# Experts with first key 96 or more: one pass of 128-expert tiles in place of gathered rows

## The reference

```
q = (hf @ w_q).reshape(n_tok, 8, 2, 128)
half_scores = einsum('thpd,hpnd->thpn', q, sub_keys)        # 8 heads, 2 x 128 keys
s_top, i_top = top_k(half_scores, 16)
cand = s_top[:, :, 0, :, None] + s_top[:, :, 1, None, :]    # 16 x 16 pairs
cand_idx = i_top[:, :, 0, :, None] * 128 + i_top[:, :, 1, None, :]
best, pos = top_k(cand, 16);  expert_idx = cand_idx at pos;  gates = softmax(best)
act = einsum('td,thkd->thk', x, u_tab[expert_idx])
out = einsum('thk,thkd->td', gates * gelu(act), v_tab[expert_idx])
```

## Time and profile before

| | us |
|---|---|
| median of 3 runs | 2410.4 (2410.38 to 2410.79) |
| profiled execution | 2410.53 |
| its span, first to last instruction | 2408.9 |
| VectorE busy | 1360.5 (56%) |
| TensorE matmuls busy | 1545.4 (64%) |
| GpSimd busy | 564.1 (23%) |
| ScalarE busy | 186.3 (8%) |
| moved by DMA | 796.21 MB, mean 331 GB/s |

### The profile page before, as it was taken

One profiled execution on the slowest core, in us unless ns is written; L12 is line 12 of the kernel. 1 busy time (PEld: TensorE's weight loads), 2 busy tenths in 40 slices (PEclk: granted clock), 3 DMA queues, 4 the chain that ended last, 5 costly groups with the idle time before them and its releaser, 6 DMA issues.

```text
span 2408.9 us, 18981 instructions
## 1 busy us (share of the span) xinstructions
PE 1545.4 (64%) x7056; PEld 975.7 (41%) x7056; DVE 1360.5 (56%) x2094; ACT 186.3 (8%) x311; POOL 564.1 (23%) x552
## 2 busy tenths in 40 slices
PE   5899899989999999898233333333334333333335
PEld 4788788878888888786000000000000000000001
DVE  7821587794354412488766566566665555455543
ACT  1122221210000000200000000000000000000000
POOL 1000000000000000023444333334344433333342
PEclk9999899999999999999555555555555555555555
DMA  9963455656566564077999999999999999999996
GB/s 393 413 259 114 194 226 234 258 230 255 233 267 255 209 244 157 35 304 282 373 421 422 421 421 421 421 422 421 421 422 421 422 422 422 421 421 421 420 422 279
DMA packets 95343, 796.21 MB, mean 331 GB/s; under 512 B 11424, under 2 KB 11424, under 8 KB 13872
## 3 DMA queue, kind: packets, MB, share of 16 engines
q0 software_dynamic: 78512, 606.14, 61.1%
q1 hardware_dynamic: 16768, 189.27, 20.1%
HBM read 791.18 MB, written 4.19 MB: 330 GB/s over the span
## 4 chain that ended last, share of the span: by engine, by line
DMA 42%; PE 39%; DVE 12%; issue 4%; POOL 1%; ACT 1%; SPq 0%; POOLq 0%; DVEq 0%
DMA arena<-expert_u,expert 39%; PE ps L606 24%; PE ps L614 9%; DVE arena L1168 6%; PE ps L630 3%; DMA arena<-expert_v,expert_q 2%; DVE mod_rows L928 1%; DMA arena<-ada_early 1%; POOL arena L413 1%; DVE work L984 1%; DVE work L981 1%; DVE work L891 0%; PE ps L769 0%; PE ps L807 0%; POOL mod_rows L413 0%
## 5 line engine op out<-in xcount | busy, mean ns | idle before, releaser
L1168 DVE CUSTOM_DVE_ANT_0 arena<-arena,buf_b 128x2048 f32<-128x2048 f32 x256 | 586.2, 2293 | 481.3 <-DMA arena<-expert_u,expert 479.7
L819 PE MATMUL ps<-arena,mod_rows 128*32 128x512 f32 x1536 | 365.2, 1047 | 591.3 <-DMA arena<-expert_v,expert_q 562.9
L413 POOL DMA_INDIRECT arena<-expert_u,expert x256 | 255.5, 998 | 895.0 <-DVE work L1168 681.7
L606 PE MATMUL ps<-buf_a,arena 128*128 128x256 f32 x1920 | 423.9, 383 | 6.1 <-DVE arena L1002 5.3
L819 PEld LDWEIGHTS ps<-arena,mod_rows 128*32 128x32 f32 x1536 | 40.1, 140 | 908.1 <-DMA arena<-expert_v,expert_q 803.5
L606 PEld LDWEIGHTS ps<-buf_a,arena 128*128 128x128 f32 x1920 | 367.3, 192 | 57.2 <-issue 6.7
L819 PE MATMUL ps<-mod_rows 128*32 128x512 f32 x512 | 120.1, 1032 | 179.6 <-DMA mod_rows<-expert_v,expert_q 179.6
L606 PE MATMUL ps<-arena 128*128 128x256 f32 x1024 | 223.7, 379 | 1.0 <-ACT arena L545 1.0
L413 POOL DMA_INDIRECT arena<-expert_v,expert_q x192 | 199.6, 1039 | 80.5 <-issue 63.5
L606 PEld LDWEIGHTS ps<-arena 128*128 128x128 f32 x1024 | 193.9, 190 | 27.3 <-issue 1.3
L400 POOL DMA_DIRECT2D arena<-ada_late x32 | 16.9, 529 | 772.4 <-DVE mod_rows L928 642.6
(11 more groups left out here) (208 smaller groups left out, 1004.5 us busy)
## 6 DMA issues: line engine op xcount, KB each, us to landing
arena<-weights SPq DMA_DIRECT2D x62, 2048.0 KB, 7.9
arena<-ada_late POOLq DMA_DIRECT2D x32, 2048.0 KB, 9.2
arena<-ada_early SPq DMA_DIRECT2D x16, 2048.0 KB, 17.1
arena<-w_early SPq DMA_DIRECT2D x8, 1536.0 KB, 8.9
arena<-expert_u,expert POOLq DMA_INDIRECT x256, 16.8
arena<-expert_v,expert_q POOLq DMA_INDIRECT x192, 18.0
buf_a<-x_t SPq DMA_DIRECT2D x1, 2048.0 KB, 20.5
arena<-ln_rows POOLq DMA_DIRECT2D x1, 2048.0 KB, 7.2
```

Source lines behind the costliest of these rows:

```text
L413: pool.indirect_dma_start(slots[row % ring], None, table, bass.IndirectOffsetOnAxis(ap=indices[:, n // HEADS, column:column + 1], axis=0))\
L606: last = mm(ps[:, bank, c * TOKENS:(c + 1) * TOKENS], ring[slot][:, first + k, c * P:(c + 1) * P], rhs[:, k, :], start=(k == 0), stop=(k = ...
L819: last = mm(ps[j * GROUP:(j + 1) * GROUP, n // HEADS * QUADS + g, :], spread_w[n % 2][:, e, :], v_slot[row % V_RING][:, j * QCOLS:(j + 1) ...
L1168: v.tensor_tensor_reduce(out=u_slot[s], in0=u_slot[s], in1=h2[:, n // HEADS], scale=1.0, scalar=0.0, op0=ALU.mult, op1=ALU.add, accum_out= ...
```

## The change

Experts whose first key is 96 or more (4096 of 16,384, 32 tiles of 128) are no longer gathered. The gathers get `bounds_check=GATHERED - 1`, so a row with a larger index is left out and the slot keeps what it held; its gate is zero in `gates_left`, which `weigh` now reads. The products of `reduce_row` no longer go over the slot but to `products`, and each `reduce_row` waits for the one before.

- **U, dense.** SyncE streams 32 tiles of 1 MB of a transposed copy `dense_u` through two slots. `dense_u_piece` multiplies a quarter of a tile with all 256 tokens (4 matmuls, 128 x 128 by 256); a whole tile's result goes through Gelu on ScalarE into `dense_act`. Four tiles come ahead of the first weights, 28 are spread over queries 1 to 5.
- **Gates.** In queries 6 to 8 the chosen keys and gates are transposed by TensorE and copied by ScalarE, so that a token is a column. For each token a column mask (second key and gate; even tokens on ScalarE, odd ones on VectorE) and a row mask (first key, 16 tokens in one instruction) are multiplied by a matmul of 32 columns (`spread_gates`), which gives the token's gates over the 32 x 128 dense experts. `weigh_dense` multiplies `dense_act` by them, 16 tokens at a time.
- **V, dense.** 32 tiles of V are streamed through the same two slots, and `dense_v_piece` adds a quarter of a tile's product (8 matmuls) in queries 10 to 14 into the same eight PSUM banks.
- **Moved.** Block 1's choices are in queries 1 to 5 (`late_choices` walks through the same `choice`, two pieces ahead of the gates of the head before). Block 0's layer norm is in query 15. The stores of `x_mid` go from SyncE's queue to GpSimd's, ahead of the gathers. `xq` is loaded after the last dense U tile. V's ring has six slots instead of eight, and its gathers follow in their order from the sixth row of query 1 on. `pe.wait_ge(s_dw, BATCHES)` holds TensorE in front of its step 9.

TensorE's loop variable n now is one above that of the rows of V which it weighs.

```diff
-U_RING, V_RING = 4, 8
+U_RING, V_RING = 4, 6
+DENSE = 32
+FIRST_DENSE = N_KEYS - DENSE
+GATHERED = FIRST_DENSE * N_KEYS
+BATCH = 512 // DENSE
+BATCHES = TOKENS // BATCH
+MASKS = 8
...
         buf_a = sb("buf_a", [P, CHUNK])
         h_t = buf_a[:].rearrange("p (k t) -> p k t", k=KT)
...
         u_slot = [arena[:, s * row:(s + 1) * row] for s in (4, 5, 6, 7)]
-        v_slot = [arena[:, s * row:(s + 1) * row] for s in (8, 9, 10, 11)] + [shift2, scale2]\
-            + [arena[:, s * row:(s + 1) * row] for s in (0, 1)]
+        v_slot = [arena[:, s * row:(s + 1) * row] for s in (8, 9, 10, 11)] + [shift2, scale2]
+        dense_slot = [arena[:, s * row:(s + 1) * row] for s in (2, 3)]
+        dense_act = [buf_a[:].rearrange("p (a t) -> p a t", t=TOKENS), arena[:, 0:CHUNK].rearrange("p (a t) -> p a t", t=TOKENS)]
         late_scores = gate1.rearrange("p (c n) -> p c n", c=2 * HEADS)
+        col_mask = gate1[:, 0:MASKS * N_KEYS].rearrange("p (r n) -> p r n", r=MASKS)
...
         level_mask = cst[:, C_LEVELS:C_IOTA]
...
+        gates_left = part(BLOCKS * SLOTS).rearrange("p (b s) -> p b s", b=BLOCKS)
+        col_t = part(TOKENS)
+        distance = [pq_t[1][:, n * N_KEYS:(n + 1) * N_KEYS] for n in range(2)]
+        products = [xr[:, 1], sk.rearrange("p c n -> p (c n)")]
...
+        EARLY_DENSE = 4
+        FIRST_MASKS = 6
+        late_steps = [(n, e) for n in range(1, 6) for e in range(1, TOPK, 2)]
+        dense_steps = [(n, e) for n in range(1, 6) for e in range(TOPK)]
+        mask_steps = [(n, e) for n in range(FIRST_MASKS, HEADS + 1) for e in range(TOPK)]
+        v_steps = [(n, e) for n in range(HEADS + 2, 2 * HEADS - 1) for e in range(TOPK)]
...
+        DENSE_U_AT = shares(dense_steps, 4 * EARLY_DENSE, 4 * DENSE)
+        DENSE_V_AT = shares(v_steps, 0, 4 * DENSE)
+        TOKENS_AT = {(FIRST_MASKS + t * 3 // BATCH // TOPK, t * 3 // BATCH % TOPK): [] for t in range(TOKENS)}
+        for t in range(TOKENS):
+            TOKENS_AT[FIRST_MASKS + t * 3 // BATCH // TOPK, t * 3 // BATCH % TOPK].append(t)
+        SOFT_AT = {late_steps[5 * h + 3]: [h] for h in range(HEADS)}
...
+            for a in range(DENSE):
+                sp.wait_ge(dense_used[a % 2], 1 + a // 2)
+                sp.dma_start(dense_slot[a % 2], dense_u[a * P:(a + 1) * P, :]).then_inc(dense_loaded[a % 2], 16)
+            sp.wait_ge(s_mid, 16 * BLOCKS)
+            for s in range(2):
+                sp.wait_ge(dense_used[s], 1 + DENSE // 2)
+            for j in range(QUADS):
+                sp.dma_start(xq[j * GROUP:(j + 1) * GROUP].rearrange("t b g c -> t (b g) c"),
+                             x_mid.rearrange("(a t) (j c) -> j t a c", t=GROUP, j=QUADS)[j]).then_inc(s_xq, 16)
+            for a in range(DENSE, 2 * DENSE):
+                sp.wait_ge(dense_used[a % 2], 1 + a // 2)
+                sp.dma_start(dense_slot[a % 2], expert_v[GATHERED + (a - DENSE) * P:GATHERED + (a - DENSE + 1) * P, :])\
+                    .then_inc(dense_loaded[a % 2], 16)
+            sp.wait_ge(s_gmm, TOKENS)
...
-            for b in range(BLOCKS):
-                sp.wait_ge(s_x1, b + 1)
-                sp.dma_start(x_mid[b * P:(b + 1) * P, :], xr[:, b]).then_inc(s_mid, 16)
-            sp.wait_ge(s_mid, 16 * BLOCKS)
...
+                                        bass.IndirectOffsetOnAxis(ap=indices[:, n // HEADS, column:column + 1], axis=0),
+                                        bounds_check=GATHERED - 1, oob_is_err=False)\
...
+            for b in range(BLOCKS):
+                pool.wait_ge(s_x1, b + 1)
+                pool.dma_start(x_mid[b * P:(b + 1) * P, :], xr[:, b]).then_inc(s_mid, 16)
...
-            wait_alone(pool, used[0], 1 + F_END[0])
-            for e in range(V_RING - 2, V_RING):
-                gather_v(0, e)
...
-                    if n > 1 or e >= V_RING:
+                    if n > 1 or e >= (TOPK - U_RING) // 2:
...
-                gelu(i)
-                nc.scalar.preload_act_table_set("natural_log_exp_and_others")
-                soft_exp(i + (HEADS + 1))
-                nc.scalar.preload_act_table_set("gelu_and_others")
...
-            nc.scalar.preload_act_table_set("gelu_and_others")
-            with me.loop(HEADS - 1, 0) as i:
-                gelu(i + (HEADS + 1))
+            def dense_gelu(a):
+                act_e.wait_ge(dense_used[a % 2], 2 + a // 2)
+                run(dense_act[a // 16][:, a % 16, :], ps[:, 4 + a % 2, 0:TOKENS], ACT.Gelu).then_inc(s_dact, 1)
...
+                t = slice(b * P, (b + 1) * P)
+                act_e.wait_ge(s_tok, b + 1)
+                run(row_t[:, t], ps[:, 6, 0:P], ACT.Copy)
+                run(col_t[:, t], ps[:, 6, P:2 * P], ACT.Copy)
+                run(minus_col_t[:, t], ps[:, 6, P:2 * P], ACT.Copy, scale=-1.0)
+                run(gate_t[:, t], ps[:, 6, 2 * P:3 * P], ACT.Copy)
...
+                if t >= MASKS:
+                    act_e.wait_ge(s_gmm, t - MASKS + 1)
+                act_e.wait_ge(s_slot, t // P + 1)
+                me.link(run(distance[t // 2 % 2], keys, ACT.Abs, bias=minus_col_t[:, t:t + 1]))
+                run(col_mask[:, t % MASKS], distance[t // 2 % 2], ACT.Relu, bias=gate_t[:, t:t + 1], scale=minus_gate_t[:, t:t + 1])\
+                    .then_inc(s_col, 1)
+            for n in range(BLOCKS * HEADS):
+                for e in range(TOPK):
+                    for h in SOFT_AT.get((n, e), ()):
+                        nc.scalar.preload_act_table_set("natural_log_exp_and_others")
+                        soft_exp(HEADS + h + 1)
+                        nc.scalar.preload_act_table_set("gelu_and_others")
+                    if n == FIRST_MASKS and e == 0:
+                        for b in range(BLOCKS):
+                            choice_by_slot(b)
+                    for a in DENSE_U_AT.get((n, e), ()):
+                        if a % 4 == 3:
+                            dense_gelu(a // 4)
+                    for t in TOKENS_AT.get((n, e), ()):
+                        if t % 2 == 0:
+                            mask_cols(t)
+                    if n == BLOCKS * HEADS - 1 and e == 13:
+                        nc.scalar.preload_act_table_set("natural_log_exp_and_others")
+                        rstd_of_groups(0, 0, QUADS)
+                        nc.scalar.preload_act_table_set("gelu_and_others")
+                if n == 0:
+                    for a in range(EARLY_DENSE):
+                        dense_gelu(a)
+                gelu(n)
             nc.scalar.preload_act_table_set("natural_log_exp_and_others")
             for g in range(QUADS):
                 rstd_of_groups(1 + g, QUADS + g, QUADS + g + 1)
...
+            def dense_u_piece(i):
+                a, q = i // 4, i % 4
+                if q == 0:
+                    pe.wait_ge(dense_loaded[a % 2], 16 * (a // 2 + 1))
+                    if a > 1:
+                        pe.wait_ge(s_dact, a - 1)
+                tile = dense_slot[a % 2].rearrange("p (k j) -> p k j", k=KT)
+                for k in range(4 * q, 4 * q + 4):
+                    last = mm(ps[:, 4 + a % 2, 0:TOKENS], tile[:, k, :], h2_t[:, k, :], start=k == 0, stop=k == KT - 1)
+                if q == 3:
+                    last.then_inc(dense_used[a % 2], 1)
...
+                a, q = i // 4, i % 4
+                t = DENSE + a
+                if q == 0:
+                    pe.wait_ge(dense_loaded[t % 2], 16 * (t // 2 + 1))
+                for r in range(2 * q, 2 * q + 2):
+                    for j in range(QUADS):
+                        last = mm(ps[j * GROUP:(j + 1) * GROUP, r, :], dense_act[a // 16][:, a % 16, r * GROUP:(r + 1) * GROUP],
+                                  dense_slot[t % 2][:, j * QCOLS:(j + 1) * QCOLS], start=False, stop=False, skip_group_check=True)
+                if i == 4 * DENSE - 1:
+                    last.then_inc(s_dv, 1)
+                elif q == 3:
+                    last.then_inc(dense_used[t % 2], 1)
...
+                if b:
+                    pe.wait_ge(s_slot, b)
+                for c in range(2):
+                    nc.tensor.transpose(ps[:, 6, c * P:(c + 1) * P], halves_of[:, c, b, :], ident)
+                nc.tensor.transpose(ps[:, 6, 2 * P:3 * P], gates[:, b, :], ident).then_inc(s_tok, 1)
...
+                i = t // BATCH
+                if t % BATCH == 0:
+                    pe.wait_ge(s_rowm, i + 1)
+                    if i > 1:
+                        pe.wait_ge(s_dw, i - 1)
+                if t % 2 == 0:
+                    pe.wait_ge(s_col, t // 2 + 1)
+                else:
+                    pe.wait_ge(s_colv, t // 2 + 1)
+                mm(ps[:, 6 + i % 2, t % BATCH * DENSE:(t % BATCH + 1) * DENSE], col_mask[:, t % MASKS], row_mask[i % 2][:, t % BATCH, :],
+                   start=True, stop=True, skip_group_check=True).then_inc(s_gmm, 1)
+            for i in range(4 * EARLY_DENSE):
+                dense_u_piece(i)
+            for n in range(1, BLOCKS * HEADS + 1):
...
+                if n == FIRST_MASKS:
```

(72 more changed lines are left out.)

87 lines of the change are left out of this document (58 added, 29 removed).

## The result

The changed kernel takes 2367.7 us (four runs, 2366.7 to 2372.6) against 2410.6 us: a ratio of 0.9826, 95% interval 0.9809 to 0.9843. It is 43 us faster where 90 were forecast. The profiled execution has a span of 2365.0 us against 2318 in the sum.

The account below looks back on a forecast made before the run. DMA transfers at 421 GB/s were taken to bound the gather phase. First weighing 1165, transfers 1044.5, uneven engines 80, query 6 entry 5 and refills, clock, masks 10 give 2304.5; plus 13.2, span 2318, forecast 2320 us; range 2240 to 2450.

Parts of the forecast that it names:

- GpSimd needs 2 x (0.94 + 0.30) = 2.5 us for a pair, under 3.66: Gather phase: GpSimd issues a pair of gathers in 2.5 us, within the 3.66 us beat where nothing dense flows.
- rival C: Gathers: the bounds test makes GpSimd slow, 5.1 us a pair, over the beat; 2435 us in all; chance 0.08.
- TensorE in queries 6 to 8: Gate stage: VectorE's masks, products and weighing at 3.95 us a row were taken to set 48 rows, 190 us.
- Term (c), uneven engines: Gather phase: 80 us added because DMA engines would be unevenly loaded when rows are left out.
- the free drift: Low end of the forecast's own range, written 2320 - 60 - 15; its explanation is not in the text given.
- the 16%: High end of the forecast's own range, 2245 to 2385 us; its explanation is not in the text given.
- D of the chances: A rival at chance 0.13, partly faster and partly slower; its description is not in the text given.
- term (e): Gather phase: 10 us added for refills, clock drops and masks.
- Term (a), the first weighing: End of the head: first weighing at 1165 us, 4 us later through the serial wait and the gates_left step.
- rival B: Gathers: a row left out is still moved or takes as long; 2558 us in all; chance 0.06.
- rival A: TensorE stays at half clock, making the kernel slower; chance 0.07.
- (b): First weighing to last landing: 420 units of plain transfers, 1044.5 us.

Follow-up runs that it names:

- even_sparse: Kernel before the change, with every fourth partition left out of every gather and reduce products written beside the slot (output wrong): 2150.2 us, ratio 0.8928.
- all_out: Kernel before the change, with a gather bound of 0, so nearly every row is left out, and products beside the slot: 2202.7 us, ratio 0.9135.
- none_out: Kernel before the change, with a gather bound that no index passes, so nothing is left out, and products beside the slot: 2411.4 us, ratio 1.0002.
- gates_32cols: Changed kernel with 32 instead of 128 stationary columns in the gate matmuls (three quarters of the dense experts get no gates): 2355.9 us, ratio 0.9766.
- sparse_only: Kernel before the change, with only rows of first key 96 or more left out of gathers and products beside the slot (output wrong): 2201.9 us, ratio 0.9126.
- after_even: Changed kernel with every fourth partition left out of the gathers instead of rows with first key 96 or more (output wrong): 2328.2 us, ratio 0.9653.
- gelu0_first: Changed kernel with ScalarE's Gelu of query 0 ahead of the last two early dense Gelus (same computation): 2355.8 us, ratio 0.9772.

## Why the prediction was right in direction and off in size

**The steps that failed.** Two steps of the prediction are wrong, and a third, the first weighing below, was overlooked. The first is "GpSimd needs 2 x (0.94 + 0.30) = 2.5 us for a pair, under 3.66". The short gather was taken as the price and the long ones of the earlier trace rows as exceptions, used only for rival C. Sustained, a gather costs GpSimd 1.9 to 2.1 us with its gap (1.91 in the last queries of even_sparse, where the DMA engines are full too, and 2.09 in all_out), so 3.8 to 4.2 us for a pair. At the old beat of 4.97 us this is hidden, which is why shows short gathers; at 3.66 us it is the bound. The kernel before already shows it in the one stretch in which GpSimd has 15 gathers to issue without a wait, just behind the first weighing, without any bounds test. They start every 1.90 us on average; the first five:

```profile
1180.06 2.47 POOL L413 DMA_INDIRECT arena<-expert_u,expert  x1 [4.35 <-DVE work L1168]
1182.84 0.94 POOL L413 DMA_INDIRECT arena<-expert_u,expert  x1 [0.30 <-issue]
1184.08 2.60 POOL L413 DMA_INDIRECT arena<-expert_v,expert_q  x1 [0.31 <-issue]
1186.98 0.93 POOL L413 DMA_INDIRECT arena<-expert_u,expert  x1 [0.30 <-issue]
1188.22 2.84 POOL L413 DMA_INDIRECT arena<-expert_v,expert_q  x1 [0.30 <-issue]
```

Rival C had the mechanism, slow gathers, but blamed the bounds test, which adds only some 0.11 us to a gather (none_out), and priced a pair at 5.1 us, over the old beat. In the stretches without dense tiles the 3.8 to 4.2 us measured are already enough to bound.

**The second failed step: TensorE in queries 6 to 8.** These were sized by VectorE alone, at 190 us; TensorE's work there was never summed. VectorE was busy 174.6 us, so its price was not too low. But TensorE was busy 207.9 of the 222.7 us: the 256 gate matmuls are 512 instructions, 119.3 us in the page (233 ns each), beside 48 rows of V at 1.93 us, 93 us. The excess is 39.4 us; gates_32cols takes 9 of it away and then, in queries 7 and 8, meets GpSimd's pace. Up to 6 us more go with the loads of xq, which fall in the first 12.2 us of query 6: there the DMA engines are at a share of 1.04 and 1.07 for 192 and 238 GB/s.

```profile
1567.80:1575.00 7.20, 4.37 (x18) 1.91 (x18) 5.57 (x8) 4.43 (x17) 2.00 (x2) 0.50 1.04 192
1575.00:1580.00 5.00, 5.00 (x24) 3.27 (x24) 4.36 (x9) 3.40 (x10) 2.78 (x2) 0.50 1.07 238
```

At 421 GB/s the same bytes need 3.9 + 2.2 us less. The forecast counted them as two units of full speed. That this time was lost to the end, and lost by these loads, is argued from these rows only.

**Term (c), uneven engines.** No run shows this term: no trace says which rows a DMA engine serves or how far the engines drift apart, so the 80 us, the free drift and the 16% at the ends of the forecast's range, and D's share of the chances were the author's estimates. What the runs show in their place is what it costs that the rows are left out at random places: leaving out every fourth partition instead is 52 us faster on the kernel before (sparse_only to even_sparse) and 38 us on the changed one (after_even; 56 if its seven extra units had cost their full price, but nearly all of them lie in stretches that other engines bound). In queries 1 to 5 and 10 to 14 it is 31.7 us on about 240 gathered units (296 less some 58 dense), 5%, under the 9% that 80 us are of 358 units. So the cost is right in kind and smaller than I reckoned, and D of the chances, which needed still more, is out. Nor does a run show the 10 us of term (e) by themselves; measured is the clock in the dense stretches, 0.93 and 0.96.

**Term (a), the first weighing.** 1177.5 instead of 1165 us. I looked at what VectorE has to do ahead of it and not at what stands in front of the Gelu of query 0 in ScalarE's program. gelu0_first moves it 15.8 us forward, to 1161.7, and the kernel is 12 us faster.

**What held.** Bytes and units (rival B is out: a left-out row is a short packet). The clock in the dense stretches, 0.93 and 0.96, so rival A is out, and TensorE is busy 81% and 79% there. (Its argument that rows without pause show the clock up is not general: query 7 has TensorE busy 69.1 of 69.1 us at 0.50.) Queries 10 to 14: 397.3 us for 151.2 units, where (b) and (c) together, 2.68 us a unit, give 405. The entry of query 6: TensorE's next row of V came 4.6 us after the weighing, 5 forecast. The tail, 12.9 us behind the last landing, 13.2 forecast. The sign of being wrong that the prediction named, a phase outside 1080 to 1210 us, did not show: it is 1174.6. And its sign for uneven engines, a DMA share under 1 in query 9 or 15, did show, where the chain has GpSimd; the sign of rival C, gathers of over 2 us, was the better one.

**The account.** Excess over plain transfers: 38 us for the places of the rows left out; about 62 us in queries 6 to 9 and 15, by their chains mostly from TensorE's gates and rows and from GpSimd's pace (39.4 + 17.0 + 11.6, less the 6.2 that after_even gives back there). The other 27 lie in the other stretches: most of them behind the first weighing, where the DMA share is 0.88 for a query (13 us), and in the tail (7.7 us). No run takes these apart. The forecast was 80, 5 and 10. A term too large by 42 us hid part of two that were too small by 57 and 17: the result was nearer than the reasons deserved, and that it lies inside the stated range is in part luck.

How much of the 62 is GpSimd's and how much TensorE's is shown by a run only for queries 6 to 8 (9 us TensorE's). No run has a faster GpSimd, so for queries 9 and 15 its part rests on the chain, and what would bound them without it stays open.

## What to carry to other kernels

When a change shortens the beat, each engine must be priced again at its sustained pace, not at the duration that it shows while it waits for others: here a gather with its gap cost 1.91 to 2.09 us sustained, and 1.24 at the old beat. The place to read it is a stretch of the old profile in which the engine never waits, however short. Leaving rows out of a gather saves bytes but no issue time, so it pays down to the issuing engine's pace, here 1.9 to 2.1 us per gather of 128 rows (2.09 with 1 GB/s moving, all_out). Each engine's work in a new stretch has to be summed, also that of an engine that had time to spare before: TensorE, 39% busy in the gather phase before, was busy 207.9 of 222.7 us in queries 6 to 8. A result that one program computes is only as early as everything ahead of it in that program: VectorE waited 17.5 us for a Gelu that stood behind four others.
